# Features of the linear attention formed within the first projection, the stick heads' norm in their block, and low halves taken by VectorE

## The reference

```
u    = rmsnorm(x) @ w_in                       # 1536 columns for stick attention, 1792 for RWKV-7
o_sb = stick_breaking(q, k, v);  o_sb = o_sb * rsqrt(mean(o_sb^2 per head) + eps) * sb_out_g
um   = u + (token_shift(u) - u) * shift_mu     # r, k, v, xw, xa, xg
decay = exp(-exp(-softplus(-(w0 + tanh(xw) @ w2)) - 0.5))
a    = sigmoid(a0 + xa @ a2);   g = sigmoid(xg) @ g2
kk   = k*k_k * rsqrt(max(sum((k*k_k)^2 per head), 1e-24));   k = k * (1 + (a-1)*k_a)
out  = rwkv7_scan(r, decay, k, v, kk, a) ... + (sum(r*k*r_k) * v);   o_rw = out * g
h    = x + concat(o_sb, o_rw) @ w_out          # then mixture of experts, final norm, second block
```

## Time and profile before

| | |
|---|---|
| median of 3 runs | 1476.79 us (1476.45 to 1480.57) |
| profiled execution | 1477.63 us, its span 1475.9 us |
| TensorE busy | 1288.1 us, 87% of the span |
| VectorE busy | 564.3 us, 38% |
| ScalarE busy | 479.1 us, 32% |
| GpSimd busy | 173.1 us, 12% |
| granted TensorE clock, mean | 0.933 |

### The profile page before, as it was taken

The page is one execution under the profiler, slowest core; times in us unless marked ns, Lnnn a source line. Parts: engine busy times, 40 slices in busy tenths (PEclk is TensorE's granted clock), DMA queues, the critical chain, the costliest instruction groups (busy, mean ns, idle before and its releaser), DMA issues. The chain is left out here.

```text
span 1475.9 us, 24366 instructions
## 1 busy us (share of the span) xinstructions
PE 1288.1 (87%) x10299; PEld 998.4 (68%) x10299; DVE 564.3 (38%) x1010; ACT 479.1 (32%) x806; POOL 173.1 (12%) x219
## 2 busy tenths in 40 slices
PE   5999797579986949998883699999989989899988
PEld 4888753269966735654442698888877767666668
DVE  3331132765653132322223513344438753522222
ACT  4222266612134221111112424555545533111120
POOL 4000032010004012322211001122200000000030
PEclk9999899789997969998987799999999999999989
DMA  4332000000017559999996346233152026113011
GB/s 144 114 100 72 1 0 0 14 3 4 4 59 287 201 193 367 386 390 394 390 405 228 90 152 135 77 100 96 58 73 71 30 91 226 57 57 114 0 58 58
DMA packets 92488, 195.53 MB, mean 132 GB/s; under 512 B 9510, under 2 KB 73084, under 8 KB 79452
## 3 DMA queue, kind: packets, MB, share of 16 engines
q1 hardware_dynamic: 86604, 183.48, 36.5%
q0 software_dynamic: 5200, 8.40, 1.8%
q10 hardware_dynamic: 576, 2.10, 0.4%
HBM read 184.74 MB, written 16.81 MB: 137 GB/s over the span
## 5 line engine op out<-in xcount | busy, mean ns | idle before, releaser
L1768 PE MATMUL hidden_ps<-w_gate,gathered_t 128*64 128x256 f32 x432 | 116.4, 430 | 24.1 <-DMA w_up<-exp_w_up_dram 23.3
L1768 PE MATMUL hidden_ps<-w_up,gathered_t 128*64 128x256 f32 x432 | 116.4, 430 | 0.0
L1768 PEld LDWEIGHTS hidden_ps<-w_gate,gathered_t 128*64 128x64 f32 x432 | 64.8, 156 | 62.6 <-issue 36.8
L1333 PE MATMUL wo_ps<-w_out_high,wo_x_high 128*128 128x256 f32 x256 | 75.2, 294 | 19.2 <-POOL wo_x_low L1374 19.2
L414 PE MATMUL proj_ps<-block_in_high,w_in_low 128*128 128x512 f32 x232 | 90.5, 390 | 0.0
L414 PE MATMUL proj_ps<-block_in_low,w_in_high 128*128 128x512 f32 x232 | 90.5, 390 | 0.0
L414 PE MATMUL proj_ps<-block_in_high,w_in_high 128*128 128x512 f32 x232 | 90.4, 390 | 0.0
L462 DVE TENSOR_TENSOR w_in_low<-w_in_raw,w_in_high 128x2048 fp32r<-128x2048 f32 x20 | 45.8, 2292 | 116.4 <-ACT w_in_high L454 116.4
L414 PE MATMUL gate_ps<-block_in_high,gate_w_high 128*128 128x512 f32 x192 | 79.8, 416 | 11.3 <-DVE gate_w_low L462 11.3
L414 PE MATMUL gate_ps<-block_in_low,gate_w_high 128*128 128x512 f32 x192 | 76.5, 398 | 0.0
L414 PE MATMUL gate_ps<-block_in_high,gate_w_low 128*128 128x512 f32 x192 | 76.3, 397 | 0.0
(11 more groups left out here) (456 smaller groups left out, 3147.2 us busy)
## 6 DMA issues: line engine op xcount, KB each, us to landing
w_gate<-exp_w_gate_dram SPq DMA_DIRECT2D x27, 1024.0 KB
w_up<-exp_w_up_dram SPq DMA_DIRECT2D x27, 1024.0 KB
w_down<-exp_w_down_dram SPq DMA_DIRECT2D x27, 1024.0 KB
w_in_raw<-w_in_dram SPq DMA_DIRECT2D x20, 1024.0 KB, 5.7
slot_scratch_and_keys<-w_in_dram SPq DMA_DIRECT2D x14, 1024.0 KB, 5.3
vb<-w_in_dram SPq DMA_DIRECT2D x6, 1024.0 KB, 5.6
gate_w_raw_odd<-w_in_dram SPq DMA_DIRECT2D x6, 1024.0 KB, 5.9
slot_scratch_and_keys<-exp_w_gate_dram SPq DMA_DIRECT2D x5, 1024.0 KB
```

The source lines that it names most:

```text
L1333: m = pe.matmul(banks[n % nb][:, 0:UNIT], x[a][k][:, c * P:(c + 1) * P], wts.parts(u, k, slice(0, UNIT))[b], start=(k == 0 and a + b == 0) ...
L1768: x = pe.matmul(g_bank[e % 2][a * CAP:(a + 1) * CAP, 0:DE], xT[e % 2][:, k, :], w[:, k, :], start=(k == 0), stop=(k == KC - 1))
```

## The change

It has three parts.

1. A class `EarlyFeatures` puts part of `rwkv_features` into `project_first`. Its methods are called between the q and k tiles: after tiles 15 and 16 (counted from 1) TensorE makes two sums of squares each, after 17 and 18 two decay products each, after 19 and 20 two rate products each, all in the two banks of `mix_ps`. ScalarE gets the tanh and sigmoid of the low-rank inputs, the squares, the eight sigmoids, and at its end `Ln` and `Exp` of the key norm, with two loads of a function table. VectorE gets the bounds, the scans, `centre` (end of chunk, two subtractions) and `keys` (normed key, the factor on k, `rate` times key). SyncE loads the two low-rank matrices behind weight unit 3. The results live in buffers that exist for longer (`mixT`, the key scratch, `b_hat`).
2. `normalize_heads` is gone as a block. `rwkv_features` holds its instructions beside what is left: the three exponentials, `kk_r`, the two hats (both by VectorE now), bonus and gate.
3. In `out_projection` ScalarE writes row 0's high half ahead of the weights' high half, the table for `Sqrt` is loaded after unit 1, and VectorE takes GpSimd's eight subtractions.

```diff
+class EarlyFeatures:
...
+    def load(self, sp):
+        sp.dma_start(self.w2[0:64, :], self.A["rw_w2"][0]).then_inc(self.loaded, 16)
+        sp.dma_start(self.w2[64:128, :], self.A["rw_a2"][0]).then_inc(self.loaded, 16)
...
+    def lora_inputs(self, act, mixed):
+        act.preload_act_table_set("sigmoid_and_others")
+        act.wait_ge(mixed, RT)
+        act.activation(self.um[0:64, 3 * FT, :], self.um[0:64, 3 * FT, :], ACT.Tanh).then_inc(self.lora, 1)
+        act.activation(self.um[:, 3 * FT + 1, :], self.um[:, 3 * FT + 1, :], ACT.Sigmoid).then_inc(self.lora, 1)
+    def squares(self, act, f):
+        if f >= 2:
+            act.wait_ge(self.summed, f - 1)
+        act.activation(self.tmp[:, f % 2, :], self.k[:, f, :], ACT.Square,
+                       scale=par_col(self.const, PARAM_AT["rw_k_k"] + f)).then_inc(self.squared, 1)
+    def sums(self, pe, f):
+        if f == 0:
+            pe.wait_ge(self.made, 10)
+        pe.wait_ge(self.squared, f + 1)
+        if f >= 2:
+            pe.wait_ge(self.bounded, f - 1)
+        pe.matmul(self.banks[f % 2][:, :], self.const["heads"][:, :], self.tmp[:, f % 2, :], start=True, stop=True).then_inc(self.summed, 1)
+    def decay(self, pe, f):
+        if f == 0:
+            pe.wait_ge(self.loaded, 32)
+            pe.wait_ge(self.lora, 1)
+        if f < 2:
+            pe.wait_ge(self.bounded, f + 3)
+        else:
+            pe.wait_ge(self.stored, f - 1)
+        pe.matmul(self.banks[f % 2][:, :], self.w2[0:64, f * P:(f + 1) * P], self.um[0:64, 3 * FT, :], start=True, stop=True).then_inc(self.product, 1)
...
+    def rates(self, pe, f):
+        pe.wait_ge(self.stored, f + 3)
+        pe.matmul(self.banks[f % 2][:, :], self.w2[64:128, f * P:(f + 1) * P], self.um[64:128, 3 * FT, :], start=True, stop=True).then_inc(self.product, 1)
...
+    def store_decay(self, act, f):
+        act.wait_ge(self.product, f + 1)
+        act.activation(self.H["sig"][:, f, :], self.banks[f % 2][:, :], ACT.Sigmoid,
+                       bias=par_col(self.const, PARAM_AT["rw_w0"] + f)).then_inc(self.stored, 1)
...
+    def store_rate(self, act, f):
+        act.wait_ge(self.product, FT + f + 1)
...
+    def inverse_norms(self, act):
+        act.preload_act_table_set("natural_log_exp_and_others")
+        kkn = self.H["kkn"]
+        act.wait_ge(self.made, 10)
+        act.wait_ge(self.bounded, FT)
+        act.activation(kkn, kkn, ACT.Ln, scale=float(2.0 ** LOG_BITS)).then_inc(self.logged, 1)
+        act.wait_ge(self.logged, 1)
+        act.activation(kkn, kkn, ACT.Exp, scale=-0.5, bias=self.const["log_shift"][:, :]).then_inc(self.rstd, 1)
...
+    def bound(self, dve, f):
+        dve.wait_ge(self.summed, f + 1)
+        dve.tensor_scalar(self.H["kkn"][:, f, :], self.banks[f % 2][:, :], 1e-24, None, ALU.max).then_inc(self.bounded, 1)
...
+        dve.wait_ge(self.stored, f + 1)
+        self.step(dve, dve.tensor_tensor_scan(self.H["cum"][:, f, :], self.starts[:, :], self.H["sig"][:, f, :], 0.0, ALU.mult, ALU.add))
+    def centre(self, dve):
+        cum3, sig3 = (self.H[n].rearrange("p f (c t) -> p (f c) t", t=CH) for n in ("cum", "sig"))
+        self.step(dve, dve.tensor_copy(self.H["ends"], cum3[:, :, CH - 1]))
+        ends = self.H["ends"].unsqueeze(2).to_broadcast([P, FT * NC, CH])
+        self.step(dve, dve.scalar_tensor_tensor(out=cum3, in0=ends, scalar=-0.5, in1=cum3, op0=ALU.mult, op1=ALU.add))
+        self.step(dve, dve.tensor_tensor(sig3, cum3, sig3, ALU.subtract))
...
+    def keys(self, dve):
+        kkn, rate = self.H["kkn"], self.H["rate"]
+        dve.wait_ge(self.rstd, 1)
+        for f in range(FT):
+            self.step(dve, dve.scalar_tensor_tensor(out=kkn[:, f, :], in0=self.k[:, f, :], scalar=par_col(self.const, PARAM_AT["rw_k_k"] + f),
+                                                    in1=kkn[:, f, :], op0=ALU.mult, op1=ALU.mult))
+        dve.wait_ge(self.stored, 2 * FT)
+        for f in range(FT):
+            x = self.tmp[:, f % 2, :]
+            self.step(dve, dve.tensor_scalar(x, rate[:, f, :], par_col(self.const, PARAM_AT["rw_k_a"] + f),
+                                             self.const["one_minus_ka"][:, f:f + 1], ALU.mult, ALU.add))
+            self.step(dve, dve.tensor_tensor(self.k[:, f, :], self.k[:, f, :], x, ALU.mult))
+        self.step(dve, dve.tensor_tensor(rate, kkn, rate, ALU.mult))
...
                     wts.load(sp, i)
+                    if i == 3:
+                        early.load(sp)
...
+                            turn = (n - RT - 1) // 2
+                            for f in ((n - RT - 1) % 2 * 2, (n - RT - 1) % 2 * 2 + 1):
+                                if n > RT and turn == 0:
+                                    early.sums(pe, f)
+                                elif n > RT and turn == 1:
+                                    early.decay(pe, f)
+                                elif n > RT and turn == 2:
+                                    early.rates(pe, f)
...
+                early.lora_inputs(act, mixed)
+                early.squares(act, 0)
+                early.squares(act, 1)
...
+                    pair = (0, 1) if j % 2 else (2, 3)
+                    for f in pair:
+                        if j == 0:
+                            early.squares(act, f)
+                        elif j in (3, 4):
+                            early.store_decay(act, f)
+                        elif j in (5, 6):
+                            early.store_rate(act, f)
                 for j in range(FU + 1, NU):
                     wts.split_high(act, j)
+                early.inverse_norms(act)
...
-                for j in range(RT // 2 + 1, NU):
-                    wts.split_low(dve, j)
+                wts.split_low(dve, 8)
+                early.bound(dve, 0)
+                early.bound(dve, 1)
+                early.bound(dve, 2)
+                early.bound(dve, 3)
+                wts.split_low(dve, 9)
+                early.scan(dve, 0)
+                early.scan(dve, 1)
+                wts.split_low(dve, 10)
+                early.scan(dve, 2)
+                early.scan(dve, 3)
+                early.centre(dve)
+                wts.split_low(dve, 11)
+                wts.split_low(dve, 12)
+                early.keys(dve)
...
+def rwkv_features(nc, A, const, um, R, H, heads):
...
+                    dve.scalar_tensor_tensor(out=R["bonus"][:, f, :], in0=r[:, f, :], scalar=par_col(const, PARAM_AT["rw_r_k"] + f),
+                                             in1=k[:, f, :], op0=ALU.mult, op1=ALU.mult).then_inc(rk, 1)
                 dve.wait_ge(ex, 1)
...
+                dve.tensor_tensor(R["kr"][:, :, 0, :], c4(kkn), c4(sig), ALU.mult).then_inc(kr, 1)
+                dve.wait_ge(ex, 2)
+                dve.tensor_tensor(R["kr"][:, :, 1, :], c4(r), c4(e1[:, :, :]), ALU.mult).then_inc(kr, 1)
                 dve.wait_ge(ex, 3)
...
+                dve.tensor_tensor(R["kh"][:, :, :], k, e2[:, :, :], ALU.mult).then_inc(hats, 1)
+                dve.tensor_tensor(rate, rate, e2[:, :, :], ALU.mult).then_inc(hats, 1)
                 for f in range(FT):
                     dve.wait_ge(bz, f + 1)
...
+                    dve.tensor_tensor(R["bonus"][:, f, :], b_bank[f % 2][:, :], vv[:, f, :], ALU.mult).then_inc(bonus, 1)
...
+                dve.wait_ge(kr, 1)
+                for f in range(FT):
+                    src, gain, dst = heads[f]
+                    dve.wait_ge(rstd, f + 1)
+                    dve.scalar_tensor_tensor(out=dst, in0=src, scalar=gain, in1=rs[:, f, :], op0=ALU.mult, op1=ALU.mult).then_inc(scaled, 1)
...
+                for f in range(2):
+                    pe.wait_ge(rk, f + 1)
+                    pe.matmul(b_bank[f][:, :], const["heads"][:, :], R["bonus"][:, f, :], start=True, stop=True).then_inc(bz, 1)
+                pe.wait_ge(loaded, 16)
                 for f in range(FT):
...
+                    pe.matmul(g_bank[f][:, :], g2[:, f * P:(f + 1) * P], um[:, 3 * FT + 1, :], start=True, stop=True).then_inc(prod, 1)
                 for f in range(FT):
...
+                    pe.wait_ge(squared, f + 1)
+                    if f >= 2:
+                        pe.wait_ge(logged, f - 1)
+                    pe.matmul(n_bank[f % 2][:, :], const["heads"][:, :], sq[:, f % 2, :], start=True, stop=True).then_inc(summed, 1)
+                for f in range(2, FT):
+                    pe.wait_ge(rk, f + 1)
+                    pe.wait_ge(bonus, f - 1)
+                    pe.matmul(b_bank[f % 2][:, :], const["heads"][:, :], R["bonus"][:, f, :], start=True, stop=True).then_inc(bz, 1)
...
+                act.preload_act_table_set("natural_log_exp_and_others")
+                act.activation(sig, sig, ACT.Exp, scale=-DECAY).then_inc(ex, 1)
+                act.activation(e1[:, :, :], cum, ACT.Exp, scale=-DECAY).then_inc(ex, 1)
+                act.activation(e2[:, :, :], cum, ACT.Exp, scale=DECAY).then_inc(ex, 1)
```

(34 more changed lines are left out.)

226 lines of the change are left out of this document (42 added, 184 removed).

## The result

| | median of the runs, us | profiled execution, us | span, us |
|---|---|---|---|
| before | 1477.00 (4 runs, 1476.45 to 1480.57) | 1477.63 | 1475.9 |
| changed | 1456.65 (4 runs, 1454.40 to 1457.42) | 1456.26 | 1454.4 |

The account below looks back on a forecast made before the run. Bounds: TensorE in the projection, an in-order ScalarE-VectorE chain in the features, GpSimd's row 0 at output projections. 14.4 - 39.7 - 0.5 - 1.9 - 0.6 = -28.3 us gave 1448.5 us; range 1446 to 1451.5 (0.65).

Parts of the forecast that it names:

- The projection, +14.4: Projection grows by 14.4 us, from twelve added float32 products and three waits on TensorE; bounds 10.3 and 17.2.
- The twelve products: In the projection, four sums, four decays and four rates on TensorE at 0.87 us each: 10.4 us.
- The waits: In the projection, TensorE stands 1.33 us for ScalarE's sigmoids, three times: 4.0 us.
- a rival, in its extreme form: Three stalls drop TensorE to 1.2 GHz for the rest of the projection: 1493.5 us; chance 0.03.
- Norm and features, -39.7: Merged norm and features block ends 18.5 us after its table load, 39.7 us less; bounds 33.8 and 41.6.
- drain behind the table load: Skill's rule of about 1.38 us per table switch, not followed; would make the features' block 1.4 us longer, 1449.9 us.
- The chunks' first products, -0.5: At the chunks' start, TensorE idles 3.9 us instead of 11.68 beforehand: 0.5 us gained; bounds 0 and 1.9.
- the first output projection, -1.9: TensorE starts at 453.5 against 455.45 in the first output projection: 1.9 us gained.
- The last output projection, -0.6: TensorE starts at 1422.9 against 1423.50 in the last output projection: 0.6 us gained.
- Elsewhere 0: Stretches outside the touched stages, such as the stick attention, were forecast to change by 0 us.

Follow-up runs that it names:

- E1: Changed kernel with ScalarE making the sigmoids of a pair of products behind the store of the tile just ahead of these products: 1445.84 us, ratio 0.9789.
- E11: E1 with each of the twelve early products made twice into the same accumulator: 1454.81 us, ratio 0.9870.
- E2: Changed kernel with six fp32r products that leave the result unchanged put ahead of each of TensorE's three waits: 1445.49 us, ratio 0.9800.
- E5: Changed kernel again, unedited, on another chip: 1452.01 us, ratio 0.9827 to the kernel before.
- E12: Changed kernel once more, unedited, on another chip than E5: 1452.21 us, ratio 0.9846 to the kernel before.

## Why the prediction was wrong

- **The projection, +14.4, measured +20.2: the step that failed.** The twelve products cost 11.4 us, not 10.4 (E1, E11): the pitch inside a run of like products was taken (0.87 us, measured 0.88), and the 0.15 us for each pair left out, which I put down to changing to them and back. The waits cost 4.1 us, forecast 4.0 (E2, and 77.6 - 73.54). What is left, 4.7 us in the first profile, is three falls of the clock at 1.57 us (E5, E12), for which the sum had nothing: it priced a wait at its length alone. I had that mechanism only as a rival, in its extreme form, to the end of the projection, at 0.03, and argued it away by a row of 250 to 257 us that kept 1.00 with longer gaps. The row was true, but one stretch in one execution; whether a wait of 1.26 us lowers the clock changes from run to run (in six profiles with the same projection, all three once, two twice, one three times). The rival should have had a short form, 0 to 3 falls of some 2 us. The Trainium skill ("TensorE: Matmul & The Clock Gate", A second HAM failure mode) was set aside on that row. It says that short idling between groups of products can make the clock swing, where it is frequent; this kernel shows the swing behind single short waits in the projection (1.00, 0.50 and 0.96 in the windows above), and not in the features' block.
- **Norm and features, -39.7, measured -39.6.** The chain was read off right, in order and in length (0.85 us of waiting for the bonus sums where 0.4 was taken), and it stays (18.62 to 18.64 us in all nine profiles that leave this block as it is). No drain behind the table load: 1.29 us from its start to the exponential.
- **The chunks' first products, -0.5, and the first output projection, -1.9:** together -2.0 in the trace. The start of the output projection moved by 2.0 us (6.80 to 4.80), forecast 1.9; at the chunks the clock had fallen all the same, so nothing was gained there.
- **The last output projection, -0.6:** 0.70 in the chain.
- **Elsewhere 0, measured +0.6:** -0.1 at the start, -1.6 in the stick attention, +0.6 up to the second block, +2.7 from there to the last projection's start (2.0, with the 0.7 above put back), and -1.0 behind it. In the second block it is the moment at which the clock rises again. Windows of before, 2.3 us behind that block's first product (821.68), and then of the changed kernel, 3.8 us behind it (799.19):

```profile
824.00:827.00 3.00, 2.44 (x11) 1.21 (x10) 2.46 (x2) 1.81 (x3) 0.00 (x0) 0.90 0.78 220
```

```profile
803.00:807.00 4.00, 3.86 (x5) 0.76 (x6) 2.67 (x3) 0.69 (x1) 0.00 (x0) 0.50 0.93 293
807.00:811.00 4.00, 4.00 (x20) 4.00 (x20) 0.23 (x1) 0.69 (x1) 0.00 (x0) 0.50 0.59 203
```

In the kernel before, 6.3 us of that block's start are at 1.2 GHz, in the changed kernel 12.8. It doesn't belong to the change: E12, the same program as the changed kernel, has 6.9 us there and takes 601.2 us to the last projection's start, as before. With no edit, stretches outside the change swing by 2 us and more each, and a sum of terms with 0 for them needs a range as wide.

What stays open: what decides, in a run, whether a wait of 1.26 us lowers the clock. No edit here steers it, and the first chip's four runs may lie high by chance or by the chip.
